# Linear attention gate between the query pairs, r projections one place sooner, and the residual constant in the norm's scale and shift

## The chip, the cores and the metric

The kernel runs on one core of one Trainium2 chip. The metric is the device time of one execution in microseconds (us). All data is float32. Each matmul of two float32 tiles appears in the trace as two matmul records.

## What is computed

The reference applies two blocks to a sequence of 256 tokens with 1024 channels. The first block is an RWKV and state-space mixer with a convolutional feed-forward. The second block has two layers, and the change lies in it. Each layer works on the tokens and on 256 context tokens, with one projection `w_in` that feeds three branches:

```python
parts = _split_cols(h @ p['w_in'] + p['b_in'])
y_a, yc_a = _gla_mixer(parts, cparts, p, last)
y_b, yc_b = _mla_mixer(parts, cparts, p, cos, sin, last)
y = _merge_branches(parts, (y_a, y_b, _conv_module(parts[9], p)), p)
...
x = _layer_norm(DN_ALPHA * x + gate1 * y, p['ln1_g'], p['ln1_b'])
x = _layer_norm(DN_ALPHA * x + gate2 * _conv_ffn(x * (1 + scale2) + shift2, p), p['ln2_g'], p['ln2_b'])
```

The gated linear attention (GLA) scans forwards and backwards over chunks. Its decay comes from a low-rank projection: log-sigmoid of `lr @ wa + ba`, for both directions. Its output is normalised and multiplied by silu(r), r being another part of the projection. In the last layer the context rows serve as keys and values only, so the kernel works there on 256 columns for queries and the residual, and on 512 columns in layer 0 (context and tokens).

## The kernel before

Activations lie transposed: 128 channels on the partitions, tokens along the free dimension. `X` holds the residual in eight tiles, `H` the modulated input of a projection. Weights stream through a ring of six slabs of eight 128x128 tiles (512 KB each). SP's queue loads them in the order in which TensorE uses them, and a slab's slot is loaded again when the job that last read it is done. POOL's queue loads, once per layer, the gate's weights and the value bias (`rowsl`, `v_bias`) and the masks (`two`).

The order of work is written out by hand, a function per engine and stage, with the prefixes `t_` (TensorE), `a_` (ScalarE), `v_` (VectorE) and `p_` (POOL). Every engine works in its own order and waits by semaphores on named steps. `open_job` gives the results of a job the next of eight PSUM banks, and waits until the last user of that bank is emptied.

Projections come in two kinds. `project` (L903) multiplies eight weight tiles straight. `t_pair` (L713, with its products at L600 or L709) computes two column blocks over two halves of the tokens with seven products instead of eight: P1, P5, P6, a, P7, c, b. VectorE forms the weight sums that it needs (`v_block_sums`, L603 to L618: S1 to S4) and the sums of the input (`v_turns`). ScalarE copies partial results out of PSUM (`a_pair_part`, L764 to L776) while the accumulation goes on in the same bank: P6 waits for the copy of P1, P7 for the copy of P6, c for the copy of P5, b for the copy of P7.

`t_gla_in`, `a_gla_in` and `v_gla_in` (L1826 to L1906) are the stage in front of the GLA. TensorE does, in this order: keys, the low-rank projection, the queries (two pairs in layer 0; four straight projections of 256 columns in layer 1, which VectorE empties at L1895), the gate projections of the context chunks (`t_gate2`, four jobs "gz" with L1928), then four value pairs (L709). ScalarE's `a_gate2` reads each gate result twice (Abs at L1944, Relu at L1945), loads the table set that has Exp and Ln (L944), and takes Exp (L1950) and Ln (L1952) of all 2048 columns at once, in place. VectorE adds the two parts (L1956). The same function runs a second time, for the token chunks, inside the units of the GLA.

`t_gla`, `a_gla` and `v_gla` (from L2048) run eight units in turn, one for each chunk and direction. A unit has decay sums (L1980), the diagonal and level products of the attention matrix (L1994, L2004, L2011), state products (L2018, L2028) and output products (L2042, L2044). Its decayed queries and keys come from ScalarE (Exp at L2105, in 14 parts), VectorE (L2143 for the differences, L2165 for the queries) and POOL (L2177 for the keys). VectorE puts the attention matrix together with masked copies (L2204, L2217), and the output products wait for these. Between the parts of a unit, `t_fill` puts one of the eight independent r projections (`t_r`, 16 matmul records of 512 columns in layer 0) and, in layer 0, a part of a conditioning matrix (`t_ada`, L1773, four slabs). Which r projection goes where is in the table `R_FILL`; `a_fill` has ScalarE's Silu of them (L2290) at the end of the same unit, or, for "start", behind the Exp parts of unit 0.

`v_ln_close` (L2973) closes a mixer or a feed-forward on VectorE: `v_coef` prepares scale and shift of the next modulation from the norm's gain and beta, then X is multiplied by ALPHA in eight instructions (L3002), then the residual is added and normalised. ScalarE writes the next `H` from the normalised X with `coef`, and `v_affine` (L3098) applies gain and beta to X itself. The function is called four times: after the mixer and after the feed-forward of each of two layers.

Of the kernel before, what the change touches and what calls it, by code (L numbers as in the profile page):

```python
# [20 lines left out]
ALU = mybir.AluOpType  # L21
ACT = mybir.ActivationFunctionType
# [3 lines left out]
DT = D // P  # L26
# [21 lines left out]
ALPHA = (2.0 * LAYERS) ** 0.25  # L48
# [190 lines left out]
class Steps:  # L239
# [5 lines left out]
    def step(self, name=None):  # L245

        self.n += 1
        if name is not None:
            self.table[name] = (self.sem, self.n)
        return 1  # L250


def build(nc, t_in, out, known):
# [3 lines left out]
    with ctx:  # L257
# [4 lines left out]
        vector_steps, scalar_steps, pool_steps = sem("vector_steps"), sem("scalar_steps"), sem("pool_steps")  # L262
        tensor_jobs = sem("tensor_jobs")
# [9 lines left out]
        def flat(a):  # L273
            return a.rearrange("p a b -> p (a b)")
# [21 lines left out]
        X = alloc(DT, 512)  # L296
        eps_col = alloc(4)
# [7 lines left out]
        def pc(key, i=0, n=1):  # L305
            c = PCOL[(key, i)] if (key, i) in PCOL else PCOL[key + (i,)]
            return par[:, c:c + n]
# [4 lines left out]
        T, A, V, G = (Steps(x, table) for x in "TAVG")  # L312
# [7 lines left out]
        def at(step):  # L320

            return step_of(step)[1]
# [59 lines left out]
        ph = alloc(9, 2, S5_TILES)  # L382
# [34 lines left out]
        gl = alloc(2, 2, 512)  # L417
# [17 lines left out]
        lsg = E.rearrange("p a b c -> p (a b c)")  # L435
# [485 lines left out]
        def bank(key):  # L921
            return ps[:, job_of[key], :]
# [19 lines left out]
        def both_tables():  # L942

            act.add_instruction(mybir.InstLoadActFuncSet(name=nc.get_next_instruction_name(), engine=mybir.EngineType.Activation, act_func_set_id=LN_EXP_SET))  # L944
# [877 lines left out]
        def hr(n):  # L1822
            return lambda k: H[:, k, 0:n]


        def t_gla_in(l, n):  # L1826
            project_across([(("k", l, m), [IN0["k"] + m * P]) for m in range(2)], "w_in_2", l, DT, hr(512), 512, lambda k: ("H", l, 0, k))
            g, s = in_pairs[l], in_src[l]
            t_pair(g, ("kp", l, 2), s, "w_in_2", l, IN0["k"] + 2 * P, IN0["k"] + 3 * P, first=True)
            project(("lr", l), "w_in_2", l, ["lr"], DT, hr(512), 512)  # L1830
            for m in range(0, 4, 2):
                if n == 512:
                    t_pair(g, ("qp", l, m), s, "w_in_2", l, IN0["q"] + m * P, IN0["q"] + (m + 1) * P)
                else:
                    for e in range(2):
                        project(("q", l, m + e), "w_in_2", l, [IN0["q"] + (m + e) * P], DT, hr(n), n)
            t_gate2(l, "c")
            for j in range(4):
                t_pair(g, ("vp", l, j), s, "w_in_2", l, IN0["v"] + 2 * j * P, IN0["v"] + (2 * j + 1) * P, product=turned_product)

# [3 lines left out]
        def a_gla_in(l, n):  # L1844
            g = in_pairs[l]
            for m in range(2):
                act.wait_ge(tensor_jobs, at(("job", ("k", l, m))))
                if m == 0:
                    act.wait_ge(vector_steps, at(("b2_free", l)))
                act.activation(kT[:, m, :], bank(("k", l, m)), ACT.Identity, bias=pc(("b_in", l, "k"), m)).then_inc(scalar_steps, A.step(("free", ("k", l, m))))  # L1850
            key, b = ("kp", l, 2), [pc(("b_in", l, "k"), m) for m in (2, 3)]
            for i, bias in enumerate((b[0], None, b[0], b[1])):
                a_pair_part(g, key, i, bias=bias)
            act.wait_ge(tensor_jobs, at(("job", (key, "b"))))
            act.activation(kT[:, 3, 0:TX], bank((key, "b"))[:, 0:TX], ACT.Identity, bias=b[1]).then_inc(scalar_steps, A.step(("free", (key, "b"))))
            table[("free", ("k", l, 3))] = table[("free", (key, "b"))]
            act.wait_ge(tensor_jobs, at(("job", ("lr", l))))
            act.activation(lr, bank(("lr", l)), ACT.Identity, bias=pc(("b_in", l, "lr"), 0)).then_inc(scalar_steps, A.step(("free", ("lr", l))))
            if n == 512:
                act.wait_ge(vector_steps, at(("q_bias", l)))  # L1860
                for m in range(0, 4, 2):
                    b = [q_bias[:, l, m + e:m + e + 1] for e in range(2)]
                    for i, bias in enumerate((b[0], None, b[0], b[1])):
                        a_pair_part(g, ("qp", l, m), i, scale=float(GDK ** -0.5), bias=bias)
            a_gate2(l, "c")
            for j in range(4):
                key = ("vp", l, j)
                for i in range(4):
                    a_pair_part(g, key, i)
                act.wait_ge(tensor_jobs, at(("job", (key, "b"))))  # L1870
                act.copy(vt[:, 0:2, (2 * j + 1) * P:(2 * j + 2) * P], token_pairs(bank((key, "b"))[:, 0:TX])).then_inc(scalar_steps, A.step(("free", (key, "b"))))
# [47 lines left out]
        def t_gate2(l, ph):  # L1919
            tiles = dict(phases(l))[ph]  # L1920
            pe.wait_ge(scalar_steps, at(("free", ("lr", l))))
            pe.wait_ge(*step_of("loaded_rowsl%d" % l))
            for d in range(2):
                for i, tt in enumerate(tiles):
                    o = open_job(("gz", l, ph, d, i))
                    p0 = 32 * d

                    ins = pe.matmul(o, lr[p0:p0 + 17, tt * P:(tt + 1) * P], rowsl[p0:p0 + 17, :], start=True, stop=True)  # L1928
                    ins.then_inc(tensor_jobs, close_job(("gz", l, ph, d, i)))

        def gate_tmp(ph):

            return lsg[:, 0:2048] if ph == "c" else flat(rg)[:, 2048:4096]

        def a_gate2(l, ph, between=None):

            lsg_ = gate_tmp(ph)
            tq = [lsg_[:, 0:512], lsg_[:, 512:1024], lsg_[:, 1024:1536], lsg_[:, 1536:2048]]
            if ph == "c" and l > 0:
                act.wait_ge(vector_steps, at(("b2_free", l)))  # L1940
            js = [(d, i) for d in range(2) for i in range(2)]
            for n, (d, i) in enumerate(js):
                act.wait_ge(tensor_jobs, at(("job", ("gz", l, ph, d, i))))
                act.activation(tq[n], bank(("gz", l, ph, d, i)), ACT.Abs).then_inc(scalar_steps, A.step())  # L1944
                act.activation(gl[:, d, i, :], bank(("gz", l, ph, d, i)), ACT.Relu, scale=-1.0).then_inc(scalar_steps, A.step(("free", ("gz", l, ph, d, i))))  # L1945
            if between is not None:
                between()
            both_tables()
            act.wait_ge(scalar_steps, A.n)
            act.activation(lsg_, lsg_, ACT.Exp, scale=-1.0).then_inc(scalar_steps, A.step())  # L1950
            act.wait_ge(scalar_steps, A.n)
            act.activation(lsg_, lsg_, ACT.Ln, bias=eps_col[:, 2:3]).then_inc(scalar_steps, A.step(("lsg", l, ph)))  # L1952
# [109 lines left out]
            t_fill(l, "end")  # L2062


        R_FILL = [{u: (u,) for u in range(8)}, {"start": (0,), 0: (1,), 2: (2, 3), 4: (4,), 5: (5,), 6: (6,), 7: (7,)}]
        ADA_FILL = {"start": 1, 1: 1, 2: 1, 3: 1, 4: 1, 5: 1, 6: 1, "end": 1}

        def t_fill(l, place):
# [894 lines left out]
        def v_coef(l, part, gain, beta):  # L2963

            a = coef[:, 2 * l + part]
            up = mod[:, l, (3 * part + 1) * DT:(3 * part + 2) * DT, :]
            by = lambda key: pc(key, 0, DT).unsqueeze(2).to_broadcast([P, DT, 2])
            ve.tensor_tensor(a[:, 0:DT, :], up, by(gain), ALU.mult).then_inc(vector_steps, V.step())
            ve.tensor_tensor(a[:, DT:2 * DT, :], up, by(beta), ALU.mult).then_inc(vector_steps, V.step())
            ve.wait_ge(vector_steps, V.n)  # L2970
            ve.tensor_tensor(a[:, DT:2 * DT, :], a[:, DT:2 * DT, :], mod[:, l, 3 * part * DT:(3 * part + 1) * DT, :], ALU.add).then_inc(vector_steps, V.step(("coef", l, part)))

        def v_ln_close(l, n, jobname, gate, tag, gain, beta, nxt):  # L2973


# [3 lines left out]
                v_turns(mix_src[l])  # L2979
            if nxt is not None:  # L2980
                v_coef(*nxt, gain, beta)

            def out_pair(m, first_done=None):
                key = ("wp", l, m)
# [13 lines left out]
                ve.scalar_tensor_tensor(out=x, in0=bank((key, "b"))[:, 0:hn], scalar=mod[:, l, gate * DT + m + 1, 0:1],  # L2998
                                        in1=x, op0=ALU.mult, op1=ALU.add).then_inc(vector_steps, V.step(("free", (key, "b"))))

            for m in range(DT):
                ve.tensor_scalar(X[:, m, 0:n], X[:, m, 0:n], ALPHA, None, ALU.mult).then_inc(vector_steps, V.step())  # L3002
            ve.wait_ge(vector_steps, V.n)

            def off_pivot(k):
# [555 lines left out]
```

## Time and profile before

| | |
|---|---|
| median of 3 runs | 2805.72 us (2803.4 to 2808.92) |
| profiled execution | 2806.23 us |
| its span | 2804.3 us |
| TensorE matmul busy | 2683.8 us, 96% |
| VectorE busy | 1826.4 us, 65% |
| ScalarE busy | 765.4 us, 27% |
| mean granted TensorE clock | 0.977 |
| DMA | 313.60 MB, 112 GB/s |

The span runs from the first to the last instruction. Busy is the time in which an engine executes; a matmul's end is modelled, so records overlap slightly. A row of the timeline has start, duration, engine, source line, operation, output and input, and a count where equal instructions are merged; in brackets stands the idle time of that engine just before it and the instruction that ended it.

### The profile page before, as it was taken

What the parts mean: (1) busy time and instruction counts of PE and PEld (TensorE: products, weight loads), DVE (VectorE), ACT (ScalarE), POOL (GpSimd) and SP (SyncE); (2) the same over time, 40 slices, a digit from 0 to 9 for tenths busy, and PEclk for the clock granted to TensorE, in tenths of its full rate; (3) what the DMA queues carried; (4) which work ended last, traced back from release to release, by engine and by line L of the source; (5) the groups of instructions that cost most, each with busy time, mean ns of one, the idle gap of its engine ahead of it and who ended that gap; (6) DMA issues with size and microseconds to landing.
All of it is one profiled execution on the core that took longest, in us unless ns stands there. A gap on an engine that the chain in (4) does not pass through costs nothing. (4 is left out here: it accounts for less than half of the span.)

```text
span 2804.3 us, 42282 instructions
## 1 busy us (share of the span) xinstructions
PE 2683.8 (96%) x16692; PEld 2149.1 (77%) x16692; DVE 1826.4 (65%) x3727; ACT 765.4 (27%) x1634; POOL 86.7 (3%) x115
## 2 busy tenths in 40 slices
PE   9979999999899999999999999999898999999997
PEld 8848789978666848664457688888597977788997
DVE  7862279743787317786946766655438738768997
ACT  2132143122553112221031433300335322223430
POOL 0000000000231000000000000000002000000000
PEclk9997999999999999999999999999999999999998
DMA  5360654432233222211222222222321242244443
GB/s 206 122 249 10 212 186 164 175 125 76 91 122 120 90 75 83 76 61 60 80 96 87 103 78 90 91 91 93 107 76 35 102 136 90 75 144 143 166 166 121
DMA packets 86739, 313.60 MB, mean 112 GB/s; under 512 B 9440, under 2 KB 11488, under 8 KB 86288
## 3 DMA queue, kind: packets, MB, share of 16 engines
q1 hardware_dynamic: 85040, 304.25, 30.7%
q0 software_dynamic: 1504, 6.64, 0.7%
q8 instruction: 135, 2.21, 0.3%
q14 instruction: 60, 0.49, 0.1%
HBM read 309.81 MB, written 1.05 MB: 111 GB/s over the span
## 5 line engine op out<-in xcount | busy, mean ns | idle before, releaser
L600 PE MATMUL ps<-sb 128*128 128x128 f32 (+1 forms) x7392 | 1152.3, 318 | 5.5 <-ACT sb L676 2.3
L600 PEld LDWEIGHTS ps<-sb 128*128 128x128 f32 x7392 | 1068.9, 191 | 91.5 <-issue 7.6
L903 PE MATMUL ps<-sb 128*128 128x256 f32 (+1 forms) x2864 | 839.9, 451 | 4.8 <-DVE sb L969 3.6
L903 PEld LDWEIGHTS ps<-sb 128*128 128x128 f32 x2864 | 542.4, 190 | 287.9 <-issue 224.7
L2822 DVE SCALAR_TENSOR_TENSOR sb<-sb 128x512 f32<-128x512 f32 (+1 forms) x480 | 275.5, 615 | 8.7
L613 DVE TENSOR_TENSOR sb<-sb 128x512 f32<-128x512 f32 x143 | 98.3, 687 | 119.5 <-PE ps L600 85.6
L772 ACT COPY sb<-ps 128x256 f32<-128x256 f32 (+1 forms) x162 | 54.6, 338 | 323.8 <-PE ps L600 256.7
L676 ACT COPY sb<-ps 128x128 f32<-128x128 f32 (+1 forms) x252 | 75.3, 299 | 219.2 <-PE ps L600 214.5
L709 PE MATMUL ps<-sb 128*128 128x128 f32 x896 | 105.1, 282 | 10.2 <-ACT sb L772 10.2
L709 PEld LDWEIGHTS ps<-sb 128*128 128x128 f32 x896 | 104.4, 198 | 12.1 <-issue 12.1
L3246 DVE SCALAR_TENSOR_TENSOR sb<-sb 128x512 f32<-128x512 f32 (+1 forms) x176 | 101.0, 615 | 15.7 <-ACT sb L3197 10.7
L615 DVE TENSOR_TENSOR sb<-sb 128x512 f32<-128x512 f32 x143 | 98.9, 692 | 4.9
L616 DVE TENSOR_TENSOR sb<-sb 128x512 f32<-128x512 f32 x143 | 97.9, 685 | 0.0
L618 DVE TENSOR_TENSOR sb<-sb 128x512 f32<-128x512 f32 x143 | 97.8, 684 | 0.0
L790 DVE TENSOR_TENSOR sb<-sb,ps 128x256 f32<-128x256 f32 (+1 forms) x84 | 31.7, 378 | 100.9 <-PE ps L600 66.3
L2177 POOL TENSOR_TENSOR sb<-sb 128x256 f32<-128x256 f32 x84 | 71.5, 889 | 393.5 <-ACT sb L2105 393.5
L916 PE MATMUL ps<-sb 128*128 128x512 f32 (+1 forms) x128 | 56.5, 606 | 16.2 <-DVE sb L3085 12.1
L2942 ACT ACTIVATE sb<-sb 128x512 f32<-128x512 f32 (+1 forms) x32 | 15.3, 522 | 198.4 <-DVE sb L3006 153.3
L1773 PE MATMUL ps<-sb 128*32 128x512 f32 x384 | 56.1, 644 | 6.4 <-DMA sb<-in_w 6.4
L916 PEld LDWEIGHTS ps<-sb 128*128 128x128 f32 x128 | 27.4, 218 | 45.1 <-issue 22.2
L2217 DVE COPY_PREDICATED sb<-sb,ps 64x128 f32<-64x128 uint32 x144 | 49.7, 345 | 11.8 <-PE ps L2011 2.3
L2105 ACT ACTIVATE sb<-sb 128x256 f32<-128x256 f32 x168 | 54.2, 414 | 4.9 <-DVE sb L2143 4.9
(428 smaller groups left out, 2694.8 us busy)
## 6 DMA issues: line engine op xcount, KB each, us to landing
sb<-in_w SPq DMA_DIRECT2D x574, 512.0 KB, 3.6
sb<-in_two POOLq DMA_DIRECT2D x2, 1088.0 KB, 7.9
sb<-in_x SPq DMA_DIRECT2D x2, 512.0 KB, 5.0
sb<-in_ctx POOLq DMA_DIRECT2D x1, 1024.0 KB, 8.0
sb<-in_v_bias POOLq DMA_DIRECT2D x2, 512.0 KB, 4.8
out_xt<-sb SPq DMA_DIRECT2D x1, 1024.0 KB, 4.8
sb<-in_par SPq DMA_DIRECT2D x1, 764.0 KB, 6.8
sb<-in_s5b POOLq DMA_DIRECT2D x1, 512.0 KB, 7.9
```

The source lines that it names most:

```text
L600: ins = pe.matmul(o, w, xs(i), start=(fresh and i == 0), stop=(i == len(ws) - 1), skip_group_check=True)
L613: ve.tensor_tensor(buf[:, 0], half(s2, 0), half(s2, 1), ALU.add).then_inc(vector_steps, V.step(("S1", key)))
L615: ve.tensor_tensor(buf[:, 1], buf[:, 0], half(s1, 0), ALU.subtract).then_inc(vector_steps, V.step(("S2", key)))
L616: ve.tensor_tensor(half(s2, 0), half(s1, 0), half(s2, 0), ALU.subtract).then_inc(vector_steps, V.step(("S3", key)))
L618: ve.tensor_tensor(buf[:, 2], half(s1, 1), buf[:, 1], ALU.subtract).then_inc(vector_steps, V.step(("S4", key)))
L676: act.copy(f.part[:, i, :], bank((key, bk))[:, 0:f.hn]).then_inc(scalar_steps, A.step((name, key)))
L709: ins = pe.matmul(o[:, tt * P:(tt + 1) * P], xs(i)[:, tt * P:(tt + 1) * P], w, start=(fresh and i == 0 and tt == 0), stop=(i == len(ws) - ...
L903: ins = pe.matmul(o[:, i * n:(i + 1) * n], w, rhs(k), start=(k == 0), stop=(k == kt - 1))
L916: ins = pe.matmul(o[j][:, i * n:(i + 1) * n], w, rhs(k), start=(k == 0 and i == 0), stop=(k == kt - 1), skip_group_check=True)
L2177: po.tensor_tensor(halves(QK[:, :, lev, :], lev, d), halves(kT[:, :, tok], lev, d), halves(E[:, :, lev, :], lev, d), ALU.mult).then_inc(po ...
L2822: ve.scalar_tensor_tensor(out=o_, in0=s_, scalar=pc(("conv_dw", l, j), m + e), in1=o_, op0=ALU.mult, op1=ALU.add).then_inc(vector_steps, V ...
L3246: ve.scalar_tensor_tensor(out=o_, in0=z2[e][:, g, 0:c, j:j + TX], scalar=pc(("ffn_dw", l, j), g * FT + m), in1=o_, op0=ALU.mult, op1=ALU.a ...
```

## The change

It has three parts. First, the gate projections of the context chunks go between the query projections, in both layers; in layer 0 ScalarE reads them between the two query pairs and takes Exp and Ln in four quarters of 512 columns, one behind each copy of the second pair. Layer 1 keeps `a_gate2` as it was. Second, in layer 0 each r projection moves one place forward. Third, ALPHA is multiplied into gain and beta of a norm once its coefficients for the next modulation are taken, so that X comes out of the norm scaled, and only the first closing still scales X.

```diff
@@ t_gla_in
                 else:
                     for e in range(2):
                         project(("q", l, m + e), "w_in_2", l, [IN0["q"] + (m + e) * P], DT, hr(n), n)
-            t_gate2(l, "c")
+                if m == 0:
+                    t_gate2(l, "c")
@@ a_gla_in
                 for m in range(0, 4, 2):
                     b = [q_bias[:, l, m + e:m + e + 1] for e in range(2)]
+                    steps = a_gate2_steps(l, "c", 4) if m else [None] * 4
                     for i, bias in enumerate((b[0], None, b[0], b[1])):
                         a_pair_part(g, ("qp", l, m), i, scale=float(GDK ** -0.5), bias=bias)
-            a_gate2(l, "c")
+                        if m:
+                            steps[i]()
+                    if m == 0:
+                        a_gate2_read(l, "c")
+            else:
+                a_gate2(l, "c")
@@ new functions
+        def a_gate2_read(l, ph):
+            lsg_ = gate_tmp(ph)
+            if ph == "c" and l > 0:
+                act.wait_ge(vector_steps, at(("b2_free", l)))
+            for n, (d, i) in enumerate([(d, i) for d in range(2) for i in range(2)]):
+                act.wait_ge(tensor_jobs, at(("job", ("gz", l, ph, d, i))))
+                act.activation(lsg_[:, n * 512:(n + 1) * 512], bank(("gz", l, ph, d, i)), ACT.Abs).then_inc(scalar_steps, A.step())
+                act.activation(gl[:, d, i, :], bank(("gz", l, ph, d, i)), ACT.Relu, scale=-1.0).then_inc(scalar_steps, A.step(("free", ("gz", l, ph, d, i))))
+
+        def a_gate2_steps(l, ph, parts):
+            w = 2048 // parts
+            def step(i):
+                cols = gate_tmp(ph)[:, i * w:(i + 1) * w]
+                if i == 0:
+                    both_tables()
+                act.wait_ge(scalar_steps, A.n)
+                act.activation(cols, cols, ACT.Exp, scale=-1.0).then_inc(scalar_steps, A.step())
+                act.wait_ge(scalar_steps, A.n)
+                act.activation(cols, cols, ACT.Ln, bias=eps_col[:, 2:3]).then_inc(scalar_steps, A.step(("lsg", l, ph)))
+            return [lambda i=i: step(i) for i in range(parts)]
@@
-        R_FILL = [{u: (u,) for u in range(8)}, {"start": (0,), 0: (1,), 2: (2, 3), 4: (4,), 5: (5,), 6: (6,), 7: (7,)}]
+        R_FILL = [{"start": (0,), 0: (1,), 1: (2,), 2: (3,), 3: (4,), 4: (5,), 5: (6,), 6: (7,)}, {"start": (0,), 0: (1,), 2: (2, 3), 4: (4,), 5: (5,), 6: (6,), 7: (7,)}]
@@
+        def part_of(gate):
+            return gate // 3
@@ v_ln_close
             if nxt is not None:
                 v_coef(*nxt, gain, beta)
+                ve.wait_ge(vector_steps, V.n)
+                for key in (gain, beta):
+                    ve.tensor_scalar(pc(key, 0, DT), pc(key, 0, DT), ALPHA, None, ALU.mult).then_inc(vector_steps, V.step())
...
-            for m in range(DT):
-                ve.tensor_scalar(X[:, m, 0:n], X[:, m, 0:n], ALPHA, None, ALU.mult).then_inc(vector_steps, V.step())
+            if (l, part_of(gate)) == (0, 0):
+                for m in range(DT):
+                    ve.tensor_scalar(X[:, m, 0:n], X[:, m, 0:n], ALPHA, None, ALU.mult).then_inc(vector_steps, V.step())
             ve.wait_ge(vector_steps, V.n)
```

## Rows read from the trace of the kernel before

**Rows 1.** The page, part 1: busy time of each engine.
```profile
PE 2683.8 (96%) x16692; PEld 2149.1 (77%) x16692; DVE 1826.4 (65%) x3727; ACT 765.4 (27%) x1634; POOL 86.7 (3%) x115
```

**Rows 2.** Timeline of TensorE, layer 0, gate projections and first value pair.
```profile
642.99 1.99 PE L1928 MATMUL ps<-sb 17*128 17x512 f32 x8
644.91 3.84 PE L709 MATMUL ps<-sb 128*128 128x128 f32 x32
653.83 6.45 PE L709 MATMUL ps<-sb 128*128 128x128 f32 x33 [5.08 <-ACT sb L772]
```

**Rows 3.** Timeline of ScalarE in the same stretch.
```profile
632.73 0.47 ACT L776 ACTIVATE sb<-ps,sb 128x256 f32<-128x256 f32 x1 [4.71 <-PE ps L600]
...
644.14 0.60 ACT L1944 ACTIVATE sb<-ps 128x512 f32<-128x512 f32 x1 [4.03 <-PE ps L1928]
...
647.50 0.67 ACT L1945 ACTIVATE sb<-ps 128x512 f32<-128x512 f32 x1
648.18 1.28 ACT L944 ACT_TABLE_LOAD   x1
649.48 1.91 ACT L1950 ACTIVATE sb<-sb 128x2048 f32<-128x2048 f32 x1
651.42 2.00 ACT L1952 ACTIVATE sb<-sb 128x2048 f32<-128x2048 f32 x1
```

**Rows 4.** Timelines of TensorE and ScalarE, layer 1, gate and value pairs.
```profile
2020.61 1.99 PE L1928 MATMUL ps<-sb 17*128 17x512 f32 x8
...
2031.51 48.20 PE L709 MATMUL ps<-sb 128*128 128x128 f32 x416 [5.14 <-ACT sb L772]
...
2029.11 2.00 ACT L1952 ACTIVATE sb<-sb 128x2048 f32<-128x2048 f32 x1
```

**Rows 5.** Timelines of TensorE, ScalarE and VectorE, layer 0, first GLA unit.
```profile
718.11 0.98 PE L2004 MATMUL ps<-sb 128*64 128x64 f32 x7 [8.55 <-DVE sb L2165]
...
715.27 0.56 ACT L2088 COPY sb<-ps 128x512 f32<-128x512 f32 x1
...
720.11 4.31 DVE L2143 TENSOR_TENSOR sb<-sb 128x512 f32<-128x512 f32 x7
```

**Rows 6.** Timelines of VectorE and TensorE, last close of the kernel.
```profile
2721.18 1.70 DVE L3002 TENSOR_SCALAR sb<-sb 128x256 f32<-128x256 f32 x8
...
2724.39 43.81 PE L600 MATMUL ps<-sb 128*128 128x128 f32 x390 [1.07 <-DVE sb L615]
```

**Rows 7.** Windows: length, busy time of each engine, clock, DMA share, GB/s.
```profile
653.80:660.30 6.50, 6.47 (x35) 6.50 (x36) 4.48 (x6) 0.53 (x2) 0.00 (x0) 0.59 0.00 0
718.10:724.60 6.50, 6.49 (x108) 6.46 (x109) 6.31 (x14) 0.05 (x1) 0.00 (x0) 0.55 0.01 4
2031.50:2038.00 6.50, 6.49 (x44) 6.50 (x45) 4.85 (x6) 0.52 (x2) 0.00 (x0) 0.76 0.00 0
2153.00:2163.00 10.00, 8.02 (x47) 7.49 (x48) 8.46 (x19) 6.06 (x16) 5.46 (x7) 0.83 0.13 50
2176.00:2183.00 7.00, 7.00 (x40) 6.97 (x39) 4.49 (x10) 1.23 (x2) 1.16 (x2) 0.61 0.00 0
```

**Rows 8.** Timeline of TensorE, two stretches without a wait.
```profile
1819.80 107.22 PE L600 MATMUL ps<-sb 128*128 128x256 f32 x496
...
2545.78 12.67 PE L600 MATMUL ps<-sb 128*128 128x128 f32 x112
```

**Rows 9.** Timeline of TensorE, layer 0, third unit.
```profile
779.41 0.46 PE L2042 MATMUL ps<-sb 128*128 128x128 f32 x2 [1.44 <-DVE sb L2217]
```

**Rows 10.** Timelines of VectorE and TensorE, layer 0, last unit.
```profile
866.68 4.82 DVE L2217 COPY_PREDICATED sb<-sb,ps 64x128 f32<-64x128 uint32 x12 [1.17 <-PE ps L2011]
...
867.51 7.13 PE L903 MATMUL ps<-sb 128*128 128x512 f32 x16
```

**Rows 11.** Timeline of TensorE, layer 1, seventh unit.
```profile
2175.73 0.77 PE L2042 MATMUL ps<-sb 128*128 128x128 f32 x2 [4.50 <-DVE sb L2217]
```

**Rows 12.** Timeline of VectorE, close of the mixer of layer 0.
```profile
1508.35 0.88 DVE L3117 SCALAR_TENSOR_TENSOR sb<-ps,sb 128x256 f32<-128x256 f32 x2 [3.89 <-PE ps L903]
```

## The prediction

> **What bounds the kernel now.** I read the page first. TensorE is busy for 96% of the span, VectorE 65%, ScalarE 27% [rows 1]. So a change to ScalarE or VectorE work is worth only what it takes out of TensorE's idle time, or out of half-clock stretches behind it. Next comes TensorE's timeline at the places that the diff touches, then the other engines' timelines for what ended each gap there, then the windows for the granted clock.
>
> Four gaps matter. In layer 0 the gate projections (L1928) stand behind the second query pair. ScalarE reads them, loads a table and runs one Exp and one Ln over 2048 columns, to 651.42 + 2.00; only then does it copy out the first product of the first value pair, and TensorE has waited 5.08 us for that [rows 2, 3]. In layer 1 the same wait is 5.14 us [rows 4]. At the start of the GLA units of layer 0 TensorE waits 8.55 us for the first decayed queries and keys [rows 5]. In the last close it waits 1.07 us for weight sums that VectorE starts behind eight scalings of X [rows 6].
>
> The first three cost more than themselves, for the clock behind them is granted at its lower level (1.2, not 2.4 GHz) for a while. A mean of 0.59 over 6.5 us loses 0.41 x 6.5 = 2.7 us in layer 0; 0.76 over 6.5 loses 1.6 in layer 1; 0.55 over 6.5 loses 2.9 behind the 8.55 us [rows 7].
>
> **Gate of layer 0.** Removed: 5.08 + 2.7 = 7.8 us. ScalarE's work now lies in the second query pair. A matmul record at 256 columns takes 107.22/496 = 0.216 us, a product of eight 1.73 [rows 8]. Let the gate projections start at 0: they take 1.92 [rows 2], P1 ends at 3.65, P5 at 5.38. The eight reads end at 647.50 + 0.67 - 642.99 = 5.18 [rows 2, 3], so the P1 copy (0.47) ends near 5.65: stall 0.3. On ScalarE follow the table load 1.28, a quarter Exp and Ln, the P5 copy, a further Exp and Ln, and P6's copy. For a quarter I take 0.65 us: 512-column reads took 0.60 to 0.67, and a quarter of 1.91 or 2.00 is the floor of 0.5 [rows 3]. Copies are 0.4 to 0.47. P6's copy then ends at 5.65 + 1.28 + 1.3 + 0.4 + 1.3 + 0.47 = 10.4. TensorE wants it for P7 behind P6 and the product into "a", at 5.65 + 3.46 = 9.1: stall 1.25. P7's copy and the fourth step lie behind later products, and the last step ends before the first value pair's P1. Kept: 1.55 us; a wait of 1.44 us had no slow stretch behind it (the next two records took 0.46 together) [rows 9]. **Gain 7.8 - 1.55 = 6.2**; bounds 0 (all of it exposed again) and 7.8.
>
> The table load lasts 1.28 from 648.18 and Exp starts at 649.48 [rows 3]. By the Trainium skill (ScalarE: Activation LUTs, What ACT_TABLE_LOAD costs) a switch costs about 2.66 us, load and drain together; the wait before P7 would then be 1.4 us longer and the whole gain 15.3, not 16.7. The row shows no drain.
>
> **Gate of layer 1.** Only TensorE's order changes: the gate projections go ahead of the last two query projections, which VectorE empties, so ScalarE is free for them. Each of these is 16 records at 256 columns, 3.5 us [rows 8], so the two are 6.9. The Ln now ends 2029.11 + 2.00 - 2020.61 = 10.5 us behind the start of the gate projections [rows 4], but P1 of the value pair is there only at 1.9 + 6.9 + 1.9 = 10.7. No wait is left. VectorE's add behind the Ln starts 7 us sooner against the pair; nothing waits for it. **Gain 5.14 + 1.6 = 6.7**; bounds 0 and 6.7.
>
> **r projections.** The first goes from unit 0 to "start", the others one place up, and unit 7 loses its own; units 0 to 6 keep one each. Start: 16 records at 512 columns, 6.9 us [rows 8, 10], fill the 8.55; 1.65 is left. The exponentials and products that end this wait are queued ahead of the new Silu, so they don't move. On ScalarE the Silu adds a table load, 0.69 and a load back: from 715.3 it ends near 717.3 and the next cumulative copy (0.56) near 717.9. VectorE takes that at 720.11 only [rows 5]: 2 us to spare. On SP's queue the slab of r0 passes four slabs of w_ada; the last of these then waits for a ring slot freed when the value pairs end and has the 6.9 us of r0 to land. POOL's queue isn't passed. Each adds nothing.
>
> Unit 7: VectorE's masked copies run from 866.68 for 4.82 us, to 871.50; r7 covers them from 867.51 [rows 10]. Without it TensorE waits 4.0 us for its output products. The clock then probably falls: a wait of 4.50 us in layer 1 [rows 11] had 0.39 x 7 = 2.7 us lost behind it, and ten microseconds in which TensorE was idle for 2 lost 0.17 x 10 = 1.7 [rows 7]. 4.0 is nearest the larger: I take 2.2, and 0.6 for the residue at the start, between 0 (the 1.44 us wait) and 1.7. Gain: 8.55 + 2.9 - 1.65 - 0.6 - 4.0 - 2.2 = 3.0; some of the 2.9 lay beside short matmuls that don't run at full rate anyway, so **2.7**. Bounds: 5.8 without half clock behind what is left, -1 if the start keeps 3 to 4 us more.
>
> **ALPHA.** Three of four groups of eight scalings go. In the last close they are 1.70 us directly ahead of the sums that TensorE waits for [rows 6]: gain, the whole 1.07. In the other two closings TensorE runs through without a wait, 107.22 us from 1819.80 and 12.67 from 2545.78 [rows 8]: nothing. Two tiny multiplications of gain and beta come into three closings. The nearest row is the scalings themselves, 1.70/8 = 0.21 each; behind them in the first closing VectorE waits 3.89 us for TensorE [rows 12], and in the other two it has lost more than that. Zero; at worst 0.5 us.
>
> **Sum.** 6.2 + 6.7 + 2.7 + 1.1 = 16.7. The profiled execution took 2806.23 (span 2804.3 and 1.9 around it), so 2789.5; the median of the runs, 2805.72, is 0.5 lower: **2789.0**.
>
> **Rivals.** (a) The fill only moves a wait: unit 7's grows by what the start loses, 2789 + 2.7 = 2792. For it: 4.0 us plus clock against 6.9. Against: the end of the masked copies is fixed by VectorE [rows 10]. 12%.
> (b) Quarters are dear: if every step loads tables twice, 8 x 1.28 = 10.2 us go back into the pair: 2799. Against: one load served both Exp and Ln [rows 3]. 10%.
> (c) The change doesn't do what it says in layer 1: banks or ScalarE come late and the wait stays, 2789 + 6.7 = 2796. Against: ScalarE there does nothing but wait. 5%.
> (d) Both gate waits stay, moved to other products: 2789 + 6.2 + 6.7 = 2802, no change that can be told. 7%.
> (e) Slower: the half clock. For waits of 5 and 8 us come waits of 0.3 to 4 us in the second query pair and the units, more in number. Each microsecond at the lower level costs half of itself: from 33 us of added half clock the gain is gone, and at 45 the kernel is at 2811.5. Against: no stretch read cost over 2.9 us [rows 7]. 4%. The Trainium skill (TensorE: Matmul & The Clock Gate, A second HAM failure mode) has just such frequent short idles make the clock swing.
> The forecast has 62%, within 2784 to 2794.
>
> **Numbers.** A measurement of this kernel can tell about 0.2%, 5.6 us, from no change. The range goes up to (b), 2799, and down to 2783: no slow clock behind unit 7 (2.2), no stall in the query pair (1.55), and the runs' spread of 2.3 below the median. Faster 62 + 12 + 10 + 5 = 89%, same 7, slower 4.
>
> **What would show it.** Right: no wait at L709 in either layer; a wait near 1.25 us inside the second query pair of layer 0, with Exp and Ln of 0.65 between its copies; 1.7 us in place of 8.55 at the first unit; a new wait of 4 us before the last unit's L2042; L3002 x8; no wait ended by L615 in the last close. Wrong: table loads between the quarters, over 3 us of stall in the query pair, over 3 at the start, or unit 7's wait well off 4.

## The result, and the profile after

The changed kernel took **2774.97 us**, median of 6 runs (2773.84 to 2788.56). In the same session the kernel before ran three times more, at 2793.36, 2789.67 and 2787.6, beside the 2803.4, 2805.72 and 2808.92 known before. The ratio of the changed kernel to all six runs of the kernel before (median 2798.38) is 0.992, 95% interval 0.9891 to 0.9948: faster by 0.8%. The median is 14.0 under the forecast of 2789.0, and 8 under the lower end of its range. Both kernels' runs turn out to be mixtures of two levels of time, so neither the ratio nor the difference from 2805.72 is what the change is worth; the experiments below separate the two. The profiled execution took 2776.32 (span 2774.5).

Lines after the diff's first hunks have moved: L1928 is now L1935, L1980 is L2012, L2004 and L2011 are L2036 and L2043, L2042 and L2044 are L2074 and L2076, L2165 and L2217 are L2197 and L2249; the quarters' Exp and Ln are L1961 and L1963.

TensorE's timeline of the changed kernel, layer 0, gate (start, length; in brackets the idle time before and what ended it), and ScalarE's beside it:

```profile
604.00 12.25 PE L600 MATMUL ps<-sb 128*128 128x256 f32 x56
616.18 1.99 PE L1935 MATMUL ps<-sb 17*128 17x512 f32 x8
618.10 7.45 PE L600 MATMUL ps<-sb 128*128 128x256 f32 x32
626.61 5.42 PE L600 MATMUL ps<-sb 128*128 128x256 f32 x24 [1.05 <-ACT sb L776]
631.86 13.34 PE L709 MATMUL ps<-sb 128*128 128x128 f32 x118
...
681.89 1.95 PE L2012 MATMUL ps<-sb 128*128 128x128 f32 x16
```

```profile
621.17 0.55 ACT L776 ACTIVATE sb<-ps,sb 128x256 f32<-128x256 f32 x1
621.74 1.28 ACT L944 ACT_TABLE_LOAD   x1
623.03 0.63 ACT L1961 ACTIVATE sb<-sb 128x512 f32<-128x512 f32 x1
623.70 0.72 ACT L1963 ACTIVATE sb<-sb 128x512 f32<-128x512 f32 x1
624.32 0.36 ACT L774 ACTIVATE sb<-ps 128x256 f32<-128x256 f32 x1
624.72 0.63 ACT L1961 ACTIVATE sb<-sb 128x512 f32<-128x512 f32 x1
625.38 0.72 ACT L1963 ACTIVATE sb<-sb 128x512 f32<-128x512 f32 x1
626.01 0.46 ACT L776 ACTIVATE sb<-ps,sb 128x256 f32<-128x256 f32 x1
```

The wait of 5.08 [rows 2] is gone; one of 1.05 is left in the second query pair, ended by P6's copy at 626.01, with one table load ahead of all quarters. The whole second pair takes 631.86 - 618.10 = 13.76, the first, of as many products, 616.18 - 604.00 = 12.18: 1.6 are kept, the wait and a shorter stop of about 0.3 for the copy of P1, which the merged row hides. The same stage in the kernel before:

```profile
618.72 24.34 PE L600 MATMUL ps<-sb 128*128 128x256 f32 x112
...
702.88 1.95 PE L1980 MATMUL ps<-sb 128*128 128x128 f32 x16
```

From the start of the query pairs to the first GLA product it is 681.89 - 604.00 = 77.9, before 702.88 - 618.72 = 84.2: **6.3**.

TensorE in layer 1, where 5.14 stood [rows 4]:

```profile
1992.42 1.99 PE L1935 MATMUL ps<-sb 17*128 17x512 f32 x8
1994.34 7.17 PE L903 MATMUL ps<-sb 128*128 128x256 f32 x32
2001.35 50.19 PE L709 MATMUL ps<-sb 128*128 128x128 f32 x448
```

448 records without a wait in 50.2 us; before, the same 448 ran from 2022.53 to 2031.51 + 48.20 [rows 4], 57.2: **7.0**. Their start before:

```profile
2022.53 3.84 PE L709 MATMUL ps<-sb 128*128 128x128 f32 x32
```

The GLA of layer 0: its start, its third unit (the same 1.44 as in [rows 9]) and its eighth, with windows behind the first and the last of the three (length, busy times, granted clock, DMA share, GB/s):

```profile
697.14 0.59 PE L2036 MATMUL ps<-sb 128*64 128x64 f32 x7 [1.70 <-DVE sb L2197]
...
759.01 0.46 PE L2074 MATMUL ps<-sb 128*128 128x128 f32 x2 [1.44 <-DVE sb L2249]
...
851.18 0.77 PE L2074 MATMUL ps<-sb 128*128 128x128 f32 x2 [4.00 <-DVE sb L2249]
```

```profile
697.10:703.60 6.50, 6.46 (x110) 5.89 (x111) 6.31 (x14) 2.18 (x3) 0.00 (x0) 0.66 0.36 144
851.10:857.60 6.50, 6.42 (x36) 6.23 (x40) 0.84 (x2) 0.00 (x0) 0.00 (x0) 0.60 0.01 3
```

8.55 has become 1.70, and the eighth unit waits 4.00, as forecast. But the granted clock is 0.66 behind the 1.70 too, and in this pair of traces the first GLA, from its first decay sum to its last output product, takes 175.5 us against 175.3 before: here the r projections gained nothing. In the last close eight scalings and the wait of 1.07 [rows 6] are gone.

```profile
2689.83 48.85 PE L600 MATMUL ps<-sb 128*128 128x128 f32 x436
```

So the waits moved as described. The two profiled executions differ by 2804.3 - 2774.5 = 29.8 us, and of these only 15.1 lie in the stretch that holds the edited code. The rest has passed before the first edited instruction runs: the query pairs start at 604.00, before at 618.72, **14.7 us** sooner in code that the change leaves alone. The windows of both kernels show where. Before, then after:

```profile
250.00:260.00 10.00, 9.83 (x77) 9.04 (x77) 3.96 (x12) 0.49 (x2) 0.00 (x0) 0.65 0.01 2
260.00:270.00 10.00, 10.00 (x69) 9.21 (x68) 3.52 (x8) 0.37 (x1) 0.00 (x0) 0.50 0.00 0
270.00:280.00 10.00, 9.14 (x90) 7.54 (x94) 0.69 (x1) 0.75 (x2) 0.00 (x0) 0.50 0.01 2
280.00:290.00 10.00, 7.95 (x31) 1.78 (x24) 0.00 (x0) 0.00 (x0) 0.00 (x0) 0.67 0.55 211
```

```profile
250.00:260.00 10.00, 10.00 (x126) 9.15 (x124) 5.95 (x15) 0.75 (x2) 0.00 (x0) 1.00 0.01 2
260.00:270.00 10.00, 6.64 (x96) 4.09 (x94) 0.69 (x1) 0.75 (x2) 0.00 (x0) 1.00 0.25 83
```

This is the serial part of the first block (small products, `t_serial`, from L1301). In the execution of before the granted clock falls to 0.50 some 3 us into it and stays there; in that of after it stays at 1.00. Both traces have nearly the same idle ahead of it. TensorE before, then after:

```profile
248.16 1.27 PE L1268 MATMUL ps<-sb 64*64 64x64 f32 x33 [1.31 <-issue]
250.17 1.16 PE L1306 MATMUL ps<-sb 64*128 64x128 f32 x8 [0.74 <-ACT sb L1286]
```

```profile
245.27 1.27 PE L1268 MATMUL ps<-sb 64*64 64x64 f32 x33 [1.04 <-issue]
247.28 1.16 PE L1306 MATMUL ps<-sb 64*128 64x128 f32 x8 [0.74 <-ACT sb L1286]
```

Whether an execution has this half-clock stretch became the question.

### The profile page after: what moved, and what is told of

The parts are those of the page before. It is cut to its first block and busy times, and to the rows that moved or that the text cites. A ratio compares the mean times of both kernels' runs of the same rounds, so it can differ in the third digit from the quotient of the medians.

```text
span 2774.5 us, 42272 instructions
## 1 busy us (share of the span) xinstructions
PE 2667.0 (96%) x16692; PEld 2135.4 (77%) x16692; DVE 1821.2 (66%) x3709; ACT 769.6 (28%) x1642; POOL 86.6 (3%) x115
## 3 DMA queue, kind: packets, MB, share of 16 engines
HBM read 309.81 MB, written 1.05 MB: 112 GB/s over the span
## 5 line engine op out<-in xcount | busy, mean ns | idle before, releaser
L3285 DVE SCALAR_TENSOR_TENSOR sb<-sb 128x512 f32<-128x512 f32 (+1 forms) x176 | 101.0, 615 | 15.7 <-ACT sb L3236 10.7
L709 PE MATMUL ps<-sb 128*128 128x128 f32 x896 | 100.4, 275 | 0.0
L2974 ACT ACTIVATE sb<-sb 128x512 f32<-128x512 f32 (+1 forms) x32 | 15.3, 522 | 197.1 <-DVE sb L3045 151.9
L2249 DVE COPY_PREDICATED sb<-sb,ps 64x128 f32<-64x128 uint32 x144 | 49.7, 345 | 11.8 <-PE ps L2043 2.4
L2074 PE MATMUL ps<-sb 128*128 128x128 f32 x192 | 42.0, 304 | 14.4 <-DVE sb L2249 14.4
```

The lines of the kernel that those rows point to most:

```text
L709: ins = pe.matmul(o[:, tt * P:(tt + 1) * P], xs(i)[:, tt * P:(tt + 1) * P], w, start=(fresh and i == 0 and tt == 0), stop=(i == len(ws) - ...
L3285: ve.scalar_tensor_tensor(out=o_, in0=z2[e][:, g, 0:c, j:j + TX], scalar=pc(("ffn_dw", l, j), g * FT + m), in1=o_, op0=ALU.mult, op1=ALU.a ...
```

## The experiments

**Each kernel again, and the change's parts alone** (e1 to e4, one chip, beside 35 runs of the kernel before). e1 is the changed kernel as it is.

> The whole change once more, beside the kernel before. Two theories for the result of 2774.97 against the 2805.72 of the first three runs of before. Theory S (stretch): some executions of either kernel carry a half-clock stretch of some 35 us in the first block (in the profiled run of before the granted clock was 0.50 from 255 to 280 us, in that of after 1.00), worth about 14 us; the change itself is worth the 16.7 of the prediction. Then the runs of both kernels fall into two groups about 14 us apart, before at about 2790 and 2805, after at about 2775 and 2789, and groups of like kind differ by 15 to 17. Theory C (change): the change's own parts brought 25 us or more; then no run of before comes under 2797 on this chip and after stays under 2780. Theory L (layout): what the change does to the program decides whether the stretch is there; then after has it in no more than one run in six again and before in nearly all.

Both kernels fall into two groups:

| | lower group | upper group |
|---|---|---|
| before, 34 runs (one more, of 2847.45, left out) | 15 runs, 2788.16 to 2797.02, median 2790.54 | 19 runs, 2802.22 to 2811.63, median 2807.85 |
| changed, 12 runs | 5 runs, 2771.76 to 2777.61, median 2775.6 | 7 runs, 2786.71 to 2793.38, median 2791.17 |
| difference | 14.9 | 16.7 |

The mean granted clock splits them as well: changed, 0.984 to 0.988 and 0.978 to 0.980. The profiled run of e1 is one of the upper group (2791.17), and its trace has the stretch at 0.50 from 250 on, in the very program that had none in the first trace:

```profile
249.34 1.57 PE L1306 MATMUL ps<-sb 64*128 64x128 f32 x8 [0.74 <-ACT sb L1286]
```

The idle ahead is 0.74 again, but these eight records take 1.57, not 1.16. Theory S holds; C and L fall (before comes under 2797, after has the stretch in 7 of 12). Only the profiled runs show the stretch itself; for the others the group is read from time and mean clock.

e2, the gates alone: `if m == 0: t_gate2(l, "c")` inside the pair loop, and the read and quarter functions.

> The gate's move alone, both layers (gate between the query pairs, quarters of Exp and Ln in layer 0), everything else as in before. The prediction's terms: 6.2 + 6.7 = 12.9 less than a run of before of the same kind (with or without the half-clock stretch at 250 to 290 us). Theory S: 12 to 14 between groups of like kind. Theory C with the surplus in the gates: 20 or more.

2790.56 (2777.65 to 2799.78, 12 runs). Lower five runs, median 2780.91, 9.6 under before's; upper six, 2794.07 to 2799.78, median 2797.2, 10.7 under; one run, 2787.06, lies between. Below the 12.9 and below the band of 12 to 14, but of the gates' size, and no surplus of 14.

e3, the fill alone:

```diff
-        R_FILL = [{u: (u,) for u in range(8)},
+        R_FILL = [{"start": (0,), 0: (1,), 1: (2,), 2: (3,), 3: (4,), 4: (5,), 5: (6,), 6: (7,)},
```

> The r projections of layer 0 one place sooner, alone. The prediction's term: 2.7 net (start gap 8.55 to about 1.7 and 2.9 of half clock behind it, less a new wait of 4.0 in the eighth unit and 2.2 of half clock behind that). After's trace showed the clock at half behind the start gap all the same, some 2.8 dearer than at full clock, so that the term would be 0.5 to 1 rather than 2.7. Theory S: within 0 to 3 of before's group of like kind. Theory C with the surplus here: 10 or more.

2806.45, ratio to before 1.0017, interval 0.9993 to 1.0041. This misses both theories' bands if read as a median, but two runs (2788.41, 2792.32) are of the lower group, eight lie between 2804 and 2813 and two between the groups (2798.88, 2801.08), so it mostly counts how often the stretch came. Like with like the gain is 0.2 in either group (the eight have a median of 2807.65, the two 2790.37). Inconclusive on 2.7 us; e10 and e11 say more.

e4, ALPHA alone (the scalings guarded by layer and mixer, gain and beta multiplied instead).

> The residual constant in scale and shift, alone. The prediction's term: 1.1 (the one wait of 1.07 in the last close, ended by the multiplication). Theory S: 0.5 to 3 less than before's group of like kind, no more. Theory C with the surplus here (48 multiplications of the three later closes no longer on VectorE): 10 or more.

2803.53, ratio 1.0003, interval 0.998 to 1.0027: inconclusive for the same reason. The traces say more: from the end of layer 1's GLA to the end of the span it is 608.4 here and 608.3 in the first trace of the changed kernel, 609.9 in before and in e2, 610.1 in e3, so about 1.5. In those three the clock also fell behind a wait of 1.78 in the last 20 us of the kernel; in e9 below, without ALPHA's edit and without this fall, it is 609.0. So ALPHA is worth 0.7 where the clock holds, and the rest is clock, which three of the four traces without the edit lost there and none of the twelve with it; whether that is the edit or chance is not shown. No part alone holds a surplus of 14 us.

**Is the stretch let in by the idle ahead of the serial part?** e5 is the changed kernel with two dummy products (the cover):

```diff
             for e in range(2):
-                pe.wait_ge(scalar_steps, at(("free", ("w", e))))
                 o = open_job(("u0", e))
+                if e:
+                    pe.matmul(o, C["ident"], tm["v"][:, 0, 0:512], start=True, stop=True)
+                pe.wait_ge(scalar_steps, at(("free", ("w", e))))
...
         def t_serial():
+            first = open_job(("su", 0))
+            pe.matmul(first, C["ident"], tm["v"][:, 0, 0:512], start=True, stop=True)
             pe.wait_ge(scalar_steps, at(("free", ("u0", 1))))
...
```

> The changed kernel with two extra 128x512 matmuls per place on TensorE whose results are overwritten: one ahead of the second of the two products that give U0 (idle 1.04 to 1.31 there in the traces), one ahead of the serial part (idle 0.74), that is just before the stretch in which the clock fell to half in some executions. Theory S1 (the fall comes from TensorE's idle just before the serial part): no run of this kernel has the stretch, all 12 lie at 2772 to 2780, and the two groups become one. Theory S2 (the small 64x64 and 64-column products of the serial part themselves, or something earlier, let the clock fall): the runs stay in two groups at about 2776 and 2790, in a similar share as before (7 of 12). If the extra matmuls only cost time: both groups up by 1 to 2.

(Each dummy is one instruction, two records in the trace; `open_job` moves ahead of the wait with it.) 2781.41, seven runs, all between 2776.05 and 2782.68: no upper group, though four of them lie above the band of 2772 to 2780. e9 and e10 repeat it on one chip with both kernels:

> The kernel before, with the same two extra matmuls at each of the two places ahead of the serial part as e5. Theory S1: its runs no longer fall into groups at 2790 and 2807, all lie at 2791 to 2798, and the difference from the changed kernel with the same cover (e10) is the change alone: 15 to 17. If the change or the program's layout decided over the stretch: before keeps it in some of the runs in spite of the cover, or the difference between the covered kernels is 25 or more.

> The changed kernel with the cover, as e5, beside e9 on the same chip. Theory S1: all runs at 2775 to 2783, 15 to 17 under e9. If the seven runs of e5 missed the stretch by luck, some come at 2790 or above.

| | runs | median, us | all runs |
|---|---|---|---|
| before, not covered | 19 | 2794.12 | 2789.18 to 2808.65, seven over 2801 |
| e9, before covered | 12 | 2793.03 | 2789.80 to 2796.37 |
| e10, changed covered | 6 | 2777.68 | 2774.89 to 2780.86 |

With the stretch out of both kernels the change is worth 2793.03 - 2777.68 = **15.35 us**. The dummies cost the kernel before nothing that these runs show: its twelve uncovered runs under 2798, from the same chip, have a median of 2793.12.

Which of the two places? e13 keeps the first dummy alone, e14 the second.

> The changed kernel with the extra matmul at the first place alone, ahead of the second product of U0 (idle 1.04 to 1.31 there before). If this idle lets the clock fall: no stretch, all runs at 2774 to 2780. If it is the idle of 0.74 ahead of the serial part: groups at about 2776 and 2790 as in e1. If both count together: the upper group is there but rarer than the 7 in 12 of e1.

> The changed kernel with the extra matmul at the second place alone, ahead of the serial part (idle 0.74). If this idle lets the clock fall: no stretch, all runs at 2774 to 2780. If it is the longer idle between the products of U0: groups at about 2776 and 2790. If both count together: the upper group is there but rarer than 7 in 12.

e13: 2787.68, 12 runs from 2775.71 to 2794.15, seven of them at 2785.92 or above, as in e1. e14: 2776.76, six runs from 2773.91 to 2778.93, none above. TensorE in e13 and then in e14:

```profile
246.93 0.27 PE L1270 MATMUL ps<-sb 64*64 64x64 f32 x1 [0.77 <-issue]
247.12 1.13 PE L1266 MATMUL ps<-sb 128*128 128x512 f32 x2
248.18 1.15 PE L1270 MATMUL ps<-sb 64*64 64x64 f32 x32
250.17 1.13 PE L1309 MATMUL ps<-sb 64*128 64x128 f32 x8 [0.84 <-ACT sb L1288]
...
252.51 0.28 PE L1332 MATMUL ps<-sb 64*64 64x64 f32 x4
252.63 0.38 PE L1328 MATMUL ps<-sb 64*64 64x64 f32 x4
```

```profile
248.76 1.27 PE L1268 MATMUL ps<-sb 64*64 64x64 f32 x33 [0.30 <-issue]
249.96 1.12 PE L1295 MATMUL ps<-sb 128*128 128x512 f32 x2
251.02 1.16 PE L1308 MATMUL ps<-sb 64*128 64x128 f32 x8
```

In e13 the 0.84 ahead of L1309 is left, and records of four grow from 0.28 to 0.38 and then 0.43 some 2.5 us behind it. In e14 the dummy stands in that place and the clock stays at 1.00 through the serial part. In all, the six kernels with the second place filled (e5, e9 to e12, e14) had the stretch in 0 of 45 runs, e1 and e13 in 14 of 24, the kernel before in 54 of 100 (its runs over 2801). The product at the second place is enough, as e14's six runs say by themselves (at 14 in 24 such a six would come in 1 case in 190). That the small products alone let the clock fall is excluded, for they are the same in both. The idle ahead of U0's second half is not needed either: in the trace of e6 below it is 0.32, and the clock fell. What the dummy does, whether it fills the idle or puts a dense product right ahead of the small ones, these runs don't separate.

Nor does the idle by itself decide. In nine traces without a dummy it is 0.74; the clock fell in seven (before, e1, e2, e4, e6, e7, e8) and stayed in two (after, e3). Where it falls varies too: from the first record behind the idle in e7, some 2.7 us behind it in before.

**The fill, without the stretch.** e11 has the gates, ALPHA and the cover, and R_FILL as before.

> The changed kernel with the cover, and the r projections of layer 0 back at the units' own ends: only the gates and ALPHA are changed. With the fill's term as predicted (2.7) this kernel is 2.7 slower than e10; with what the traces of the changed kernel show (start gap 8.55 to 1.70, so 6.9, less 2.8 of half clock behind it that stayed, less 6.3 in the eighth unit, plus what of before's own half clock behind the start gap went) it is within 1.5 of it; if the fill loses, it is faster than e10.

2781.10 (eight runs, 2778.49 to 2784.81) against e10's 2777.68: **3.4** for the fill. With six and eight runs that spread over 6 us each, this can be off by more than 2. In the traces the first GLA's stretch, from its first decay sum to its last output product, is 172.8 in e10 and 175.3 in e11: 2.5. The start in e10, then in e11:

```profile
700.79 0.59 PE L2040 MATMUL ps<-sb 128*64 128x64 f32 x7 [1.70 <-DVE sb L2201]
...
701.25 2.97 PE L2047 MATMUL ps<-sb 128*64 128x32 f32 x95
```

```profile
700.72 0.98 PE L2040 MATMUL ps<-sb 128*64 128x64 f32 x7 [8.54 <-DVE sb L2201]
...
701.51 5.26 PE L2047 MATMUL ps<-sb 128*64 128x32 f32 x95
```

Behind 1.70 the clock stayed full in this execution and fell in the first trace of after (0.66). It fell in e5 as well and stayed in the other seven traces with this wait of 1.70. That chance is worth 2.7 us: the first GLA takes 175.5 in after and in e5, and 172.7 to 173.0 in e1, e10, e13 and e14.

**Can the waits that are left be filled?** Three edits of the tables:

```diff
 e6  ADA_FILL = {"start": 2, 1: 1, 2: 1, 3: 1, 4: 1, 5: 1, 7: 1}
 e7  R_FILL[0] = {"start": (0,), 0: (1,), 1: (2,), 3: (3,), 4: (4,), 5: (5,), 6: (6,), 7: (7,)}
 e12 ADA_FILL = {"start": 1, 1: 1, 2: 1, 3: 1, 4: 1, 5: 1, 6: 1, 7: 1}   (and the cover)
```

> The changed kernel with two of the eight 1.9 us slices of the next modulation placed where the first GLA's waits are: one more at the start (wait 1.70 at 697.14 and about 2.8 of half clock behind it), that of the end into the eighth unit (wait 4.00 at 851.18 and 2.3 of half clock behind it), that of the seventh unit to the start. If the waits and the half clock after them are the whole cost: 1.7 + 2.8 + 1.9 = up to 6.4 less, 2 to 4 if the clock still falls in the eighth unit; the first GLA's stretch from its first D product to its last O product, 173.0 to 175.5 in the two traces of the changed kernel, comes to 168 to 172. Rival: the slice placed at the start delays what the wait was for or the next units, and nothing is won (174 to 176).

> The changed kernel with the fourth to eighth r projection put back into units 3 to 7, so that unit 2, which has the second gate, is left without one and the eighth unit has its own again. If the prediction's new wait in the eighth unit (4.00, and 2.3 of half clock) is due to the missing projection alone and the gate's products and one modulation slice cover unit 2: 4 to 6 less than the changed kernel of like kind. Rival: a unit without a projection waits wherever it is; the wait appears in unit 2 (4 or more) and the time stays within 2 of the changed kernel's.

> The changed kernel with the cover and the last modulation slice of 1.9 us taken from the end of the first GLA into its eighth unit, the start as it is. In e6 that slice took the wait in the eighth unit from 4.00 with half clock behind it to 1.12 with full clock, but the slice put at the start waited 2.9 for its weights from DMA. If both hold singly: 1.9 of the wait is filled by work that is done anyway, 1 more of wait goes, and 2.3 of half clock go, so 4 to 5 less than e10. Rival: the slice in the eighth unit delays what follows or waits for its weights there: within 1 of e10.

e6: 2787.7 of 12 runs; its lower five have a median of 2778.71, not under the changed kernel's. Its stretch is 176.0. The new slice at the start waits for its weights, the seventh unit, which has lost its slice, waits 1.12, and the eighth still waits 2.18, with a granted clock of 0.74 over the 6.5 us behind it. (The expectation of e12 above takes the seventh unit's 1.12 for the eighth's.)

```profile
707.42 1.05 PE L1773 MATMUL ps<-sb 128*32 128x512 f32 x4 [2.02 <-DMA sb<-in_w]
...
862.72 0.67 PE L2074 MATMUL ps<-sb 128*128 128x128 f32 x2 [2.18 <-DVE sb L2249]
```

e7: 2790.05 of 12 runs, lower five at a median of 2776.78. The wait is gone from the eighth unit and stands in the third, longer:

```profile
770.99 3.78 PE L2060 MATMUL ps<-sb 128*128 128x256 f32 x8 [6.07 <-ACT sb L2142]
775.10 0.77 PE L2074 MATMUL ps<-sb 128*128 128x128 f32 x2 [0.32 <-DVE sb L2249]
```

The rival is right for the one unit tried: the wait goes with the missing projection. e12, with only the last slice moved to where nothing else is ready, came out at **2773.34** (six runs, 2773.10 to 2774.97), 4.3 under e10, as expected, ratio to before 0.9909 (0.9885 to 0.9933). Its eighth unit:

```profile
850.89 0.46 PE L2078 MATMUL ps<-sb 128*128 128x128 f32 x2 [2.19 <-DVE sb L2253]
```

1.8 of the wait is filled, and the first row takes 0.46, not 0.77: the clock does not fall behind 2.19 in this execution, where behind e6's 2.18 at the same place it did. So how much of the 4.3 holds in every execution is open. The median is under both kernels', and under the 2775.6 of the changed kernel's lower group, taken on another chip.

**Were the quarters needed?** e8 runs Exp and Ln of layer 0's gate whole, right behind the reads.

```diff
-                        if m:
-                            steps[i]()
                     if m == 0:
-                        a_gate2_read(l, "c")
+                        a_gate2(l, "c")
```

> The changed kernel with Exp and Ln of layer 0's gate each in one instruction of 2048 columns right after the four reads, ahead of the second query pair's copies, as in layer 1. ScalarE is then busy from the reads (617.3 to 621.2 in the changed kernel's trace) through a table load of 1.28 and some 2.3 + 2.6 to about 627.4, and the pair's first copies come after: TensorE's stall of 1.05 at 626.61 becomes about 3, so 2 more, 4 with half clock behind it. If the quarters were not needed: within 1.

2797.28, 12 runs from 2791.62 to 2802.39. That is 6 over the upper group of e1, and no run lies near 2782, where a lower group would be: all twelve seem to have had the half-clock stretch, at odds that were 7 in 12 for e1. Its one trace has it; why the share is so high stays open, so this edit's program, or its session, may shift the odds. TensorE, and what it waited for:

```profile
643.02 11.38 PE L600 MATMUL ps<-sb 128*128 128x256 f32 x40 [5.30 <-ACT sb L776]
```

```profile
638.57 1.91 ACT L1979 ACTIVATE sb<-sb 128x2048 f32<-128x2048 f32 x1
640.51 2.00 ACT L1981 ACTIVATE sb<-sb 128x2048 f32<-128x2048 f32 x1
642.42 0.46 ACT L776 ACTIVATE sb<-ps,sb 128x256 f32<-128x256 f32 x1
```

A stall of 5.30 against 1.05, and 40 records in 11.38, where 40 x 0.216 = 8.6 is full clock: 4.25 + 2.8 = 7. From the start of the query pairs to the first GLA product it is 84.4, 6.5 over the 77.9 of after, in line with the run times. I had expected 3 for the stall: the pair's first copy now also comes behind the load, so TensorE stops two products sooner.

## Why the prediction was wrong

**Gate of layer 0: right.** 6.2 forecast, 6.3 in the first pair of traces; between the covered e9 and e10 it is (690.62 - 607.37) - (685.54 - 607.66) = 5.4, as e9 lost less clock behind its wait (its 416 records took 48.32, not 49.22). Both stalls came as worked out: 1.55 forecast, 1.6 kept, and one table load served all quarters.

**Gate of layer 1: right.** 6.7 forecast, 7.0 measured, no wait left.

**r projections: right in the net where the clock holds at the start.** 2.7 forecast, 3.4 measured (2.5 in the traces). Of the 2.9 for half clock behind the old 8.55, the rows of e10 and e11 show (0.98 - 0.59) + (5.26 - 2.97) = 2.7. The new wait of 4.0 is there, with 0.40 x 6.5 = 2.6 of half clock behind it for the 2.2. The residue of 0.6 at the start is nothing in most traces and 2.7 in two, after and e5; there the whole term is gone (175.5 against 175.3). A value between two levels stood for a chance.

**ALPHA: right in kind.** 1.1 forecast, 0.7 to 1.6 in the traces by what the clock does at the end; too little for run times to show.

**Sum.** 16.7 forecast. Like with like it is 14.9 and 16.7 (e1) and 15.35 (covered).

**The step that failed** is the base and its spread: "the median of the runs, 2805.72, is 0.5 lower", and at the lower end "the runs' spread of 2.3 below the median". Three runs within 5.5 us were taken for the kernel's whole spread. The profiled execution had the half-clock stretch, and by their times so had all three; it comes in 54 of 100 later runs of the kernel before and is worth 14 to 17. The forecast of 2789.0 is the changed kernel's time with the stretch (its one such run of the first six took 2788.56, e1's upper median is 2791.17); its median of 2774.97 is without. The trace had it all along: 0.65, 0.50, 0.50, 0.67 in the windows from 250 to 290, in a stretch that the diff does not touch, which I therefore did not weigh. That other executions lack it, this one trace could not say; more runs could, and with them a second level some 14 lower, at even odds, belonged in the range. Why only one of the first six runs of the changed kernel had it stays open; with the odds of e1 (7 in 12), one or none in six is a matter of 1 case in 20.

Luck had its part in the number. The same program's twelve runs in e1 have a median of 2787.97, inside the range and 1 from the forecast. That would have been no better founded: either median tells mostly how many of its runs had the stretch.

**The rivals.** (a) to (d) did not come; where the r projections gained nothing, it was by the clock behind 1.70, and not by a longer wait in the eighth unit as in (a). (e) had the right kind of mechanism, half clock behind short idle, in the wrong place and with the wrong sign for this comparison. The Trainium skill (TensorE: Matmul & The Clock Gate, A second HAM failure mode) describes a clock that swings where TensorE idles briefly and often. The traces here show a narrower case: behind one and the same idle of 0.74 the clock stays or falls, and 14 us hang on it. With the switch of about 2.66 us that the Trainium skill (ScalarE: Activation LUTs, What ACT_TABLE_LOAD costs) states, the gain was estimated at 15.3, and run times of 14.9 to 16.7 can't tell that from 16.7. The rows can: Exp starts 0.01 behind the load (621.74 + 1.28, then 623.03), no drain, and the gate's term needs none.

## What to carry to other kernels

Before a forecast is set against a median, look through the whole trace for half-clock stretches that the change does not touch, and ask whether every run has them; price each as a second level of the time. To measure a small change in such a kernel, compare groups of like clock, or take the stretch out of both versions with a dummy product; in an idle that is there anyway it cost nothing that the runs of e9 show. A filler moved to cover one wait uncovers another unless what it leaves was free: look for work that stands where nothing waits (here the slice at the end) and move that.

## What the runs showed of the hardware

The clock's fall is not fixed by the program: the same instructions with the same idle of 0.74 ahead kept full clock in some executions and ran at 0.50 for some 30 us in others, 14 to 17 us apart in 2790. One 128x512 product of 1.1 us in that idle ended it: 0 of 45 runs had the stretch against 54 of 100; the same product at the idle 3 us earlier did nothing (7 of 12). Nor does the length of a wait fix it. Behind 1.70 at the start of the first GLA the clock fell in two traces (after, e5) and stayed in eight; behind some 2.2 in its eighth unit it fell in e6 (2.18) and stayed in e12 (2.19). Behind 4.00 there it fell in every trace; behind 1.44 in the third unit, and 1.12 in the seventh of e6, it stayed.
